# The second phase of a streaming encoder layer in two stages: gated values tile by tile, then the output product for pairs of tiles with seven half-size products

## What is computed

```python
mod = jax.nn.silu(c) @ w_ada + b_ada
shift, scale, gate = jnp.split(mod[:, None, :], 3, axis=-1)
h = _rmsnorm(x, norm_g) * (1.0 + scale) + shift
rq, rk, rv, rg, aq, ak, av, ag = _in_proj(h, w_in)
...
r_out = _head_norm(r_out).reshape(B, L, RET_WIDTH).astype(x.dtype) * jax.nn.silu(rg)
...
a_out = _swa_prompt(aq, ak, av, sink)
...
a_out = a_out * jax.nn.silu(ag)
y = jnp.concatenate([r_out, a_out], axis=-1) @ w_out
x = x + gate * y
```

## Time and profile before

| | us |
|---|---|
| median of 3 runs | 1877.16 |
| lowest, highest | 1875.1, 1878.53 |
| the profiled execution: its own time | 1879.75 |
| its span, first to last instruction | 1878.0 |
| TensorE busy in it | 1811.4 (96%) |
| VectorE, ScalarE, GpSimd busy | 1158.3, 533.6, 114.3 |
| mean granted TensorE clock, of full speed | 0.985 |

### The profile page before, as it was taken

The page is one execution under the profiler, slowest core; times in us unless marked ns, Lnnn a source line. Parts: engine busy times, 40 slices in busy tenths (PEclk is TensorE's granted clock), DMA queues, the critical chain, the costliest instruction groups (busy, mean ns, idle before and its releaser), DMA issues.

```text
span 1878.0 us, 30820 instructions
## 1 busy us (share of the span) xinstructions
PE 1811.4 (96%) x9636; PEld 1499.0 (80%) x9636; DVE 1158.3 (62%) x2742; ACT 533.6 (28%) x1471; POOL 114.3 (6%) x278
## 2 busy tenths in 40 slices
PE   6899999999999999999699999999999999999995
PEld 3678888888888888888578888888888888888884
DVE  3655666556566655667566676666666666666664
ACT  3312212212221221223332333333333333333321
POOL 1000000000000000010000000000000000000000
PEclk8999999999999999999899999999999999999998
DMA  9655555555555555554667567557567567566573
GB/s 373 226 153 141 128 149 144 128 140 139 136 134 148 145 125 144 136 152 131 186 176 211 158 172 210 158 174 206 162 177 198 166 181 192 167 186 190 160 187 102
DMA packets 489513, 314.23 MB, mean 167 GB/s; under 512 B 349554, under 2 KB 424498, under 8 KB 488452
## 3 DMA queue, kind: packets, MB, share of 16 engines
q1 hardware_dynamic: 489476, 313.77, 60.0%
HBM read 183.31 MB, written 130.36 MB: 167 GB/s over the span
## 4 chain that ended last, share of the span: by engine, by line
PE 90%; issue 4%; DMA 3%; DVE 1%; SPq 1%; POOL 0%; ACT 0%; POOLq 0%; DVEq 0%; ACTq 0%
PE bank L1245 78%; PE bank L1439 3%; PE bank L1418 3%; PE bank L1343 1%; PE bank L1335 1%; PE bank L1341 1%; PE bank L1329 1%; DMA xn_scratch<-xn 1%; DMA aqk_row<-aqk_scratch 1%; SPq L402 1%; PE bank L1398 0%; DMA xp<-xn_scratch 0%; SPq L489 0%; DMA out_gate<-gate_scratch 0%; POOL small L621 0%
## 5 line engine op out<-in xcount | busy, mean ns | idle before, releaser
L1245 PE MATMUL bank<-wh,hh 128*128 128x512 f32 x1584 | 400.9, 395 | 15.3 <-DVE k_row L904 6.1
L1245 PE MATMUL bank<-wl,hh 128*128 128x512 f32 x1584 | 393.2, 391 | 0.0
L1245 PE MATMUL bank<-wh,hl 128*128 128x512 f32 x1584 | 393.1, 390 | 0.0
L1245 PEld LDWEIGHTS bank<-wh,hh 128*128 128x128 f32 x1584 | 294.4, 190 | 77.3 <-issue 12.3
L1245 PEld LDWEIGHTS bank<-wl,hh 128*128 128x128 f32 x1584 | 298.6, 189 | 62.3
L1245 PEld LDWEIGHTS bank<-wh,hl 128*128 128x128 f32 x1584 | 298.3, 188 | 62.0
L703 ACT ACTIVATE hf<-xn,tiny_a 128x128 f32<-128x128 f32 (+1 forms) x248 | 98.6, 480 | 374.0 <-DVE xn L879 374.0
L1172 DVE SCALAR_TENSOR_TENSOR a_gate<-a_gate,bank 128x128 f32<-128x128 f32 x132 | 29.1, 283 | 205.8 <-ACT a_gate L836 205.8
L775 ACT ACTIVATE s_row<-p_in,tiny_b 128x256 f32<-128x256 f32 x264 | 130.9, 500 | 49.8 <-DVE tiny_b L1082 49.8
L1245 PE MATMUL bank<-wh,yh 128*128 128x512 f32 x528 | 133.1, 395 | 6.9 <-DVE yl L1113 6.9
L1245 PE MATMUL bank<-wl,yh 128*128 128x512 f32 x528 | 130.4, 389 | 0.0
(11 more groups left out here) (159 smaller groups left out, 2289.9 us busy)
## 6 DMA issues: line engine op xcount, KB each, us to landing
p_scratch<-s_row SPq DMA_DIRECT2D x264, 128.0 KB, 2.2
p_in<-p_scratch SPq DMA_DIRECT2D x66, 512.0 KB, 4.4
xt<-in_x_prompt SPq DMA_DIRECT2D x64, 512.0 KB, 3.8
h_scratch<-hf SPq DMA_DIRECT2D x33, 512.0 KB, 2.9
hf<-h_scratch SPq DMA_DIRECT2D x33, 512.0 KB, 4.7
out<-xt SPq DMA_DIRECT2D x32, 512.0 KB, 4.9
xn_scratch<-xn SPq DMA_DIRECT2D x31, 512.0 KB, 2.9
xp<-xn_scratch SPq DMA_DIRECT2D x124, 128.0 KB, 3.1
```

Source lines behind the costliest of these rows:

```text
L1245: ins = mm(out, a[:, k, :], b[:, k, :], start=first and n == part[0] and k == chunks[0], stop=last and n == part[-1] and k == chunks[-1])
```

## The change

**First phase.** The gate pieces are loaded one per slot in slots 0 to 3 and used in slot 4. `load_prep` and `store_prep` (slots 4 to 12) load `w_out` in four chunks of 1 MB; DVE forms three-term sums of its quarters, ACT and DVE split them, and 3.5 MB a chunk (seven 512 x 512 weight blocks, high and low) is stored to `wst_dram`. From slot 5 on the retention half of y is turned here: a load by blocks, a DVE transpose and a store to `yrt_dram` for tile t - 5. The loads of two later weight pieces move from slot 1 to slot 13.

**Second phase, by tile.** The output product, its operands and the final steps leave `slot_b`. The scores are masked in place in PSUM and ACT reads them there, writing the exponentials into `p_in`. The gated values go to `ya_dram`. `weigh` is one slot later than before. DVE now makes both parts of h (`split_hb`). GpSimd issues loads of the seven weight blocks, eight of 1 MB during tiles 2 to 7, 30 and 31, six of 1 MB after the last gate product.

**Third stage, by pair.** For two tiles p, with y as 2 x 2 blocks (two tiles of 128 rows, two halves of 512 columns) and `w_out` as 2 x 2 blocks of 512, seven products of 12 matmuls of 512 columns give both tiles' output (Strassen's method in Winograd's form), instead of 96 matmuls. DVE makes the operands' sums and low parts and the sums of the products and multiplies by the gate; ACT makes high parts, one copy and the squares; GpSimd adds to x. The 64-row sample tile keeps its 48 matmuls.

```diff
+                if not pe_turns(i, t) and (not static(i) or t < SAMPLE):
                     wait(sp, k_stored, 16 * t)
                     wait(sp, x_turned, t)
                     load_blocks(k_in, k_dram[t], k_loaded)
+                if not static(i) or t >= YR_LAG:
+                    wait(sp, yr_turned, t - YR_LAG + 1)
+                    sp.dma_start(yrt_dram[t - YR_LAG], yr_rows).then_inc(yrt_stored, 16)
+                if static(i) and t < 4:
+                    load_piece(sp, FIRST_GATE + t)
...
+                c, second = prep_chunk(i, u)
+                if second == 1:
+                    store_prep(c, 1)
+                c, second = prep_chunk(i + (u + 1) // 2, (u + 1) % 2) if static(i) else (None, None)
+                if second == 0:
+                    load_prep(c)
+                if static(i) and t == 13:
+                    sp.wait_ge(prep_lo, 8)
                     for n in range(B_KV, B_Q + 1):
                         load_piece(sp, n)
                 if static(i) and t == NT - 2:
...
+            def load_prep(c):
+
+                sp.wait_ge(ada_used, KC + 4)
+                if c:
+                    sp.wait_ge(prep_lo, 2 * c)
+                sp.dma_start(prep_raw[:, 0, :], w_out_r[:, c, COLS:D]).then_inc(prep_loaded, 16)
...
+            def store_prep(c, second):
+
+                sp.wait_ge(prep_lo, 2 * c + second + 1)
+                first, blocks = (4, 3) if second else (0, 4)
+                for low in range(2):
+                    sp.dma_start(wst_dram[low, first:first + blocks, :, c, :].rearrange("b p n -> p b n"),
+                                 prep_out[:, 4 * low:4 * low + blocks, :]).then_inc(prep_stored, 16)
...
-                if mid:
-                    for half in range(2):
-                        wait(sp, exp_done, 2 * (t - 1) + half + 1)
-                        store_blocks(p_dram[2 * (t - 1) + half], s_row[:, half], p_stored[half])
-                    p_back(*prev, 0)
+                    sp.dma_start(v_news[u][0:HALF, :], cache_v[HALF:P, :]).then_inc(newer_loaded, 16)
+                if back:
+                    p_back(*same, 0)
+                    gate_out(*same)
+                    p_back(*same, 1)
+                if not static(i) or t >= 3:
+                    ya_out(*older)
...
+                if back:
+                    gate_in(*same)
...
                 if front:
                     aqk_out(i, u)
                 if mid:
-                    p_back(*prev, 1)
-                    wait(sp, gate_scaled, t)
-                    store_blocks(g_dram[t - 1], a_gates[1 - u][:, :].rearrange("p (b n) -> p b n", b=4), g_stored)
+                    p_out(*prev, 0)
                 if front:
                     aqk_in(i, u)
...
+                if static(i) and t in early_at:
+                    pool.wait_ge(prep_stored, 4 * 64)
+                    pool.wait_ge(zb_ready, 3 * 2)
+                    load_block(*EARLY[early_at[t]], early_w_loaded)
+                if static(i) and t == SAMPLE + 2:
+                    pool.wait_ge(zb_ready, 3 * (SAMPLE + 1))
+                    for n in (2, 4, 3):
+                        for low in range(2):
+                            load_block(n, low, late_w_loaded[n])
...
+            def add_x(i, u, n):
+
+
+                p = 2 * i + u
+                xq = xqs[u]
+                src, at = ((c22f, D + COLS), (c11f, 0), (u3f, D), (u2f, COLS))[n]
+                wait(pool, gated, 4 * p + n + 1)
+                wait(pool, xq_loaded[u], 32 * i + 32)
+                nc.gpsimd.tensor_tensor(xq[:, at:at + COLS], xq[:, at:at + COLS], src, ALU.add).then_inc(added, 1)
...
+            def rms(i, u):
+
+                p = 2 * i + u
+                wait(pool, squared, 4 * p + (2 if static(i) and p == LAST else 4))
+                nc.gpsimd.tensor_tensor(out_ms, out_ssq[:, 0:2], out_ssq[:, 2:4], ALU.add).then_inc(rms_step, 1)
...
+                wait(act, sink_step, 2 * n - 1)
+                wait(act, pt_done, n - 2)
                 for j in range(4):
                     h = 4 * half + j
-                    nc.scalar.activation(s_row[:, half].rearrange("p b (j s c) -> p b j s c", j=4, s=2)[:, :, j, :, :],
-                                         p_in[:, half, j, :].rearrange("p (s b c) -> p b s c", s=2, b=4), ACT.Exp,
+                    src = s_banks[2 * half + j % 2][:, (j // 2) * 2 * P:(j // 2 + 1) * 2 * P]
+                    nc.scalar.activation(p_in[:, half].rearrange("p b (j s c) -> p b j s c", j=4, s=2)[:, :, j, :, :],
+                                         src.rearrange("p (s b c) -> p b s c", s=2, b=4), ACT.Exp,
                                          bias=s_bias[:, h:h + 1], scale=SCORE_SCALE, accum_out=row_sum[:, h:h + 1])
-                wait(act, sarg_done, n)
...
                 for j in range(4):
                     h = 4 * half + j
                     src = s_banks[2 * half + j % 2][:, (j // 2) * 2 * P:(j // 2 + 1) * 2 * P]
-                    last = V.tensor_tensor_reduce(out=p_in[:, half, j, :], in0=src, in1=m, scale=1.0, scalar=MASKED,
+                    last = V.tensor_tensor_reduce(out=src, in0=src, in1=m, scale=1.0, scalar=MASKED,
...
             def turn_p(i, u, half):
                 t = 2 * i + u
                 wait(dve, p_loaded[half], 16 * (t + 1))
+                wait(dve, pv_ready, 2 * (t - 1) + half + 1)
                 V.transpose(s_row[:, half].rearrange("p b n -> p (b n)"),
...
+                if n == 5:
+                    V.tensor_tensor(s1f, a21, a22, ALU.add).then_inc(raw_done[5], 1)
+                elif n == 6:
+                    wait(dve, raw_done[5], p + 1)
+                    wait(dve, raw_done[3], p)
+                    V.tensor_tensor(s2f, s1f, a11, ALU.subtract).then_inc(raw_done[6], 1)
...
+            def low(i, u, n):
+                p = 2 * i + u
+                wait(dve, op_hi[n], p + 1)
+                raw = ops_raw[n] if n in ops_raw else operand_in(u, n)
+                V.tensor_tensor(ops[n][1], rows4(raw), ops[n][0].bitcast(F32), ALU.subtract).then_inc(op_lo[n], 1)
...
+            def gate_mult(ap, half, count):
+
+                wait(dve, summed, count)
+                V.tensor_tensor(ap, ap, out_gate[:, half * COLS:(half + 1) * COLS], ALU.mult).then_inc(gated, 1)
+
+            def out22(i, u):
+                p = 2 * i + u
+                wait(dve, prod[7], p + 1)
+                wait(dve, summed, 7 * p + 1)
+                wait(dve, added, 4 * (p - 1) + 3)
+                V.tensor_tensor(u3f, u2f, prod_bank[7][:, :], ALU.add).then_inc(summed, 1)
+                wait(dve, prod[5], p + 1)
+                wait(dve, summed, 7 * p + 2)
+                V.tensor_tensor(c22f, u3f, prod_bank[5][:, :], ALU.add).then_inc(summed, 1)
+                V.tensor_tensor(u2f, u2f, prod_bank[5][:, :], ALU.add).then_inc(summed, 1)
+                gate_mult(c22f, 1, 7 * p + 3)
+
+            def out11(i, u):
+                p = 2 * i + u
+                wait(dve, prod[2], p + 1)
+                wait(dve, added, 4 * (p - 1) + 2)
+                V.tensor_tensor(c11f, m1f, prod_bank[2][:, :], ALU.add).then_inc(summed, 1)
+                gate_mult(c11f, 0, 7 * p + 5)
...
+            def final(i, u):
+                p = 2 * i + u
+                wait(dve, rms_step, 3 * p + 3)
+                for n in range(1 if static(i) and p == LAST else 2):
+                    x = xqs[u][:, n * D:(n + 1) * D]
+                    V.scalar_tensor_tensor(x, x, out_rstd[:, n:n + 1], fin_g[:, :], ALU.mult, ALU.mult).then_inc(fin_done, 1)
...
+                p = 2 * i + u
+                wait(pe, op_hi[n], p + 1)
+                wait(pe, op_lo[n], p + 1)
+                n_w = weights or n
+                if static(i) and p == 0:
+                    pe.wait_ge(*{1: (aq_done, SAMPLE + 1), 6: (kv_done, SAMPLE + 1), 5: (ag_done, SAMPLE + 1)}.get(
+                        n_w, (exp_done, 2 * (SAMPLE + 1))))
+                elif n_w == 7:
+                    wait(pe, squared, 4 * p)
+                elif n_w == 1:
+                    wait(pe, m1_kept, p)
+                else:
+                    read = {6: 1, 5: 4, 2: 5, 4: 6, 3: 7}[n_w]
+                    wait(pe, summed, 7 * (p - 1) + read)
...
+            last = SAMPLE // 2
+            pe.wait_ge(early_w_loaded, 8 * 16)
+            product(0, 0, 1).then_inc(prod[1], 1)
+            product(0, 0, 6).then_inc(prod[6], 1)
+            scores(last, 0)
+            product(0, 0, 5).then_inc(prod[5], 1)
+            product(0, 0, 7).then_inc(prod[7], 1)
+            weigh(last - 1, 1)
+            for n in (2, 4, 3):
+                pe.wait_ge(late_w_loaded[n], 32)
+                product(0, 0, n).then_inc(prod[n], 1)
...
+                    product(i, u, 1).then_inc(prod[1], 1)
+                    product(i, u, 6).then_inc(prod[6], 1)
+                    if static(i) and p == 1:
+                        weigh(last, 0)
+                    product(i, u, 5).then_inc(prod[5], 1)
```

(4 more changed lines are left out.)

1122 lines of the change are left out of this document (715 added, 407 removed).

## The result

| | before | after |
|---|---|---|
| median | 1876.22 us | 1941.53 us |
| lowest, highest | 1875.1, 1878.53 | 1940.16, 1949.07 |
| profiled span | 1878.0 | 1938.4 |

A forecast was written before the change was run, and what follows sets the result against it. TensorE, busy for 96% of the span, was taken as the bound. The terms -43.5 + 13.5 - 15 - 6 + 12 + 2.5 + 0 + 10 = -26.5 us gave a median of 1851 us, range 1815 to 1890.

The forecast's parts named there:

- rival 5: Matmul products: saved matmuls save no time because each costs more than 0.227 us; 0.259 cancels 43.5; chance 0.04 with others.
- The tile loop: Second phase, about 30 steady slots: 17.9 us a slot against 17.35 of TensorE work, +13.5 us, bounds 0 and +54.
- rival 3: Tile loop bound by main memory at the second p_in load behind the gate's stores, about 1905 us; chance 0.14.
- The ring: Tile loop: chain from mask through exp, gate, stores and p_in load to the next mask, 17.5 to 17.9 us.
- Four slot ends at half of it: Weight preparation, slots 5 to 12: each slot end costs half a 6.1 us stall, +12 us, bounds 0 and +24.
- rival 4: Weight preparation: all eight groups of transfers stall TensorE in full, 49 us in place of 12, 1888 us; chance 0.05.
- The gate pieces: Early first phase: loading one w_ada gate piece per slot removes a TensorE stall, -6 us, bounds 0 and -9.
- The start: Start of second phase: key/value and query products cover part of the wait for keys, -15 us, bounds -8 and -23.
- The factor of 1.36: Cost of an idle TensorE microsecond at the second phase's start, lower clock included: 27.0 / 19.8.
- The change of stages: Between tiles and pairs, with the end: new waits and shorter final product offset each other, 0, bounds -8 and +12.
- The pair loop: Third stage: GpSimd adds hold VectorE for half their length, 19.7 us a pair, +10 us, bounds 0 and +43.
- the closer of my two sums: Pair loop: VectorE's work per pair without holds, 16.6 us by distances between starts; the longer sum is 17.7.

The follow-up runs named there:

- e3: Changed kernel with the weight-preparation transfers at every second slot's end issued one slot later, behind the transfers that turn x; 1951.2 us, ratio to before 1.0389.
- e5: Changed kernel with the weight-preparation transfers in portions of 0.5 to 1 MB at three to four places per slot, same bytes; 1938.9 us, ratio to before 1.0328.
- e13: Changed kernel with weight preparation in small portions over 16 slots instead of 8, two later weight pieces in slots 22 and 23; 1927.6 us, ratio to before 1.0285.
- e6: Changed kernel with SyncE issuing both p_in loads ahead of the gate's stores and the load of h in the tile loop; 1917.9 us, ratio to before 1.0210.
- e2: Changed kernel with VectorE splitting h ahead of turning the gate in the tile loop; 1949.8 us, ratio to before 1.0375.

## Why the prediction was wrong

**What bounds, and the matmuls** were right. The 192 matmuls give 43.5 us, and the pitch did not change: 84 in 19.04 us are 0.227 each (rival 5 fell).

**The tile loop** failed by its size: +13.5 against +60.1. The mechanism stood in the text as rival 3, down to the place, the second load of p_in behind the gate's stores, and its point of 18.8 us a tile was passed (18.87). The ring is the term that failed, and it was mis-sized in several places. I led it from the exp through the gate's silu and scaling; it goes through SyncE's queue instead: four stores of the second half, the load of h, the first load of p_in, the gate's stores, 6.0 us from 1246.94 to 1252.92. The landing was taken as 4.4 and was 5.5, by the load of h ahead of it and not, as I had feared, by the rate. The first tiles and the last, where the weight blocks, the last retention tiles and `cache_k` move, cost 1.6 and 1.1 us more a tile (7 and 3 tiles). TensorE's own work is 17.7 a tile, so even a free ring would have cost +10 and not 0. Two sums were also wrong as they stand: 17.9 - 17.35 is 0.55 and not 0.45, so my own ring gives +16.5, and rival 3's 60 us more lead from 1851 to 1911 and not to 1905.

**The first phase**: "Four slot ends at half of it" was the wrong step. The three slot ends with a load behind the stores cost 7.0 to 8.0 each, in full, and the 2 MB in mid-slot, which I had left out, 1.6 to 3.0. And e3 and e5 show that grouping was not the main cause. 33.6 lies between my bound of 24 and rival 4's 49. The rate of transfers, which I had worked out for the tile loop and not here, was the number to look at: 138 GB/s before, 210 after, and half of the loss went with half of the preparation's rate (e13). The gate pieces gave 9.9 for my 6, beyond my bound of 9.

**The start** came out inside its bounds (-9.3 for -15), with a wait of 11.17 for my 5.7: the round trip is not "still as long", but now spans 8.41 of work and 11.17 of wait where it was 14.15 of wait. Why was not tried. The factor of 1.36 was too high: at the prices of the earlier trace rows the matmuls of the earlier trace rows's window are 41.0 us of work and TensorE was busy for 45.17, so the lower clock cost 4.2 and not 7.2, and an idle microsecond 24.0 / 19.8 = 1.21. A granted clock that is a mean over idle time too can't be multiplied by the busy time.

**The change of stages** was put at 0 with +12 as the bound and took about 14, what is left of the sum less slot 31. I named the six blocks as something to be covered, not as something that covers nothing for others.

**The pair loop** was right in mechanism, VectorE held by the adds, but the size, 19.8 for 19.7, is luck: two errors cancel. The holds take 3.1 us a pair and not 2.0, since the add was taken as 1.0 us and is 1.67, and the rest of VectorE's work is 19.8 - 3.1 = 16.7, the closer of my two sums and not the 17.7 that I added the 2.0 to.

The range failed since it let one of rivals 3 and 4 come true but not both in part, with the change of stages on top. The first is a matter of the order on SyncE's queue (e6), the second in half of the rate (e13). Tile loop, preparation and change of stages make 46.6, 21.6 and about 14 of the 86.9 us by which the forecast was off.

## What to carry to other kernels

A method that saves matmuls and pays with round trips through main memory shortens the time in which these trips were hidden. Walk every ring from tile to tile including the issuing queue, instruction by instruction, and work out GB/s per stage before and after. When the engine that bounds waits for an instruction, ask what that one's own engine waited for: moving the named instruction (e2) gained nothing, reordering two loads on the queue (e6) gained over 20 us. A part that rides along, here the spreading of four loads, can be the only part worth keeping.

## What was not expected of the hardware

- A GpSimd add of 128 x 512 elements took 1.67 us and one of 256 columns 1.12 beside VectorE, against 0.40 for 128 columns and 0.20 for 4: more than the 1.6 ns a column that the short ones suggest. The shortest took 1.28 and 0.73, 2.1 ns a column between them; the longer ones started behind a VectorE pass as described above, so a part of their time may be GpSimd being held.
- In the first phase TensorE had no idle time at 138 and 179 GB/s, 8 us of 260 at 195 and 24 at 210, with the queues busy for 0.53, 0.66, 0.73 and 0.77: well before they were full. In the tile loop of e6 it had next to none (1.8 us of 370) at 229 and 0.81.
- The median landing of a 0.5 MB load moved from 4.5 to 5.4 us by another 0.5 MB load issued just ahead of it.
